# Two transformer blocks on one Trainium2 core: the second block on tokens that aren't normed, first gathers routed by one head

## The reference

```python
def second_block(x, ...):
    xn = rmsnorm(x, norm1_w); proj = xn @ w_in
    gq, gk, gv, ggate, gr, mq, mk, mv = jnp.split(proj, offsets, axis=-1)
    log_a = log_sigmoid(gr @ gla_w_alpha + gla_b_alpha) / 16
    o_gla = rmsnorm(gla_chunked(gq, gk, gv, log_a), gla_out_norm_w) * silu(ggate)
    qh, kh = rope(rmsnorm(mq, q_norm_w)), rope(rmsnorm(mk, k_norm_w))   # 8 heads of 64
    mixed = concatenate([o_gla, moba_attention(qh, kh, mv)]) * mix_scale
    x = x + mixed @ w_out
    return x + peer_ffn(rmsnorm(x, norm2_w), w_query, subkeys, u_tab, v_tab)
def peer_ffn(xt, ...):
    q = (xt @ w_query).reshape(T, 8, 2, 128); s = einsum('thpd,hpkd->thpk', q, subkeys)
    sv, si = top_k(s, 16)                       # best 16 of 128 keys, per head and half
    cand = sv[:, :, 0, :, None] + sv[:, :, 1, None, :]     # 256 candidates
    top_s, pos = top_k(cand, 16); expert = cand_id[pos]; gate = softmax(top_s)
    act = gelu(einsum('thkd,td->thk', u_tab[expert], xt))
    return einsum('thk,thkd->td', gate * act, v_tab[expert])
```

## Time and profile before

| what | us |
|---|---|
| median of 3 runs (lowest, highest) | 1672.82 (1672.74, 1673.08) |
| profiled execution, its own time | 1673.72 |
| its span | 1671.9 |
| TensorE busy | 1479.3 (88%) |
| VectorE busy | 786.0 (47%) |
| ScalarE busy | 267.4 (16%) |
| POOL busy | 308.8 (18%) |

### The profile page before, as it was taken

One profiled execution on the slowest core, in us unless ns is written; L12 is line 12 of the kernel. 1 busy time (PEld: TensorE's weight loads), 2 busy tenths in 40 slices (PEclk: granted clock), 3 DMA queues, 4 the chain that ended last, 5 costly groups with the idle time before them and its releaser, 6 DMA issues.

```text
span 1671.9 us, 17113 instructions
## 1 busy us (share of the span) xinstructions
PE 1479.3 (88%) x6432; PEld 810.1 (48%) x6432; DVE 786.0 (47%) x1839; ACT 267.4 (16%) x651; POOL 308.8 (18%) x288
## 2 busy tenths in 40 slices
PE   6999999899999999999699798898787778887768
PEld 5897885644444434443446575553333333333323
DVE  2216754522232323222333466376767676666544
ACT  1312221100000000000133321222212121212111
POOL 0001000100000000000000012355444444444441
PEclk9999999999999999999799899999989998989999
DMA  9532347399999999999405138899999999999996
GB/s 372 238 121 89 144 152 302 132 407 427 428 428 427 428 427 428 425 429 427 194 29 224 51 139 304 312 366 422 421 422 422 421 422 420 423 422 421 422 421 278
DMA packets 60274, 551.08 MB, mean 330 GB/s; under 512 B 8608, under 2 KB 8896, under 8 KB 10400
## 3 DMA queue, kind: packets, MB, share of 16 engines
q1 hardware_dynamic: 22192, 277.47, 40.1%
q0 software_dynamic: 38000, 272.50, 39.8%
HBM read 548.90 MB, written 1.05 MB: 329 GB/s over the span
## 4 chain that ended last, share of the span: by engine, by line
PE 46%; DMA 42%; issue 5%; DVE 4%; ACT 2%; POOL 2%; SPq 1%; DVEq 0%; POOLq 0%
DMA ring<-expert_w_d 17%; DMA ring<-peer_uv_d,work 17%; PE ps L1497 8%; PE ps L1134 8%; DMA consts_sb<-peer_uv_d,work 7%; PE ps L1746 6%; PE ps L1244 5%; PE ps L1128 5%; PE ps L1605 4%; DMA ring<-w_ada_d 2%; PE ps L1401 1%; PE ps L1536 1%; POOL ring L1881 1%; PE ps L1142 1%; PE ps L1481 1%
## 5 line engine op out<-in xcount | busy, mean ns | idle before, releaser
L1746 PE MATMUL ps<-ring,work 128*128 128x512 f32 x752 | 366.1, 641 | 93.7 <-ACT work L1077 93.7
L1746 PEld LDWEIGHTS ps<-ring,work 128*128 128x128 f32 x752 | 150.3, 205 | 303.9 <-issue 180.8
L2767 DVE CUSTOM_DVE_ANT_0 ring<-ring,work 128x1024 f32<-128x1024 f32 x188 | 229.7, 1223 | 129.1 <-DMA ring<-peer_uv_d,work 127.7
L1881 POOL DMA_INDIRECT ring<-peer_uv_d,work x188 | 209.1, 1112 | 280.4 <-PE ps L1746 190.6
L1497 PE MATMUL ps<-ring,work 128*64 128x512 f32 x1024 | 225.4, 593 | 10.2 <-DMA ring<-expert_w_d 9.4
L1497 PEld LDWEIGHTS ps<-ring,work 128*64 128x64 f32 x1024 | 78.0, 137 | 154.3 <-issue 153.2
L1077 ACT ACTIVATE work<-consts_sb,work 128x128 f32<-128x128 f32 x256 | 82.7, 390 | 259.8 <-DVE work L2776 256.0
L1134 PE MATMUL ps<-ring,hT 128*128 128x512 f32 (+1 forms) x288 | 122.6, 584 | 1.7 <-issue 0.8
L1536 PE MATMUL ps<-ring,work 128*64 128x512 f32 x512 | 113.4, 595 | 0.7 <-DVE work L2397 0.7
L1746 PE MATMUL ps<-work 128*128 128x512 f32 x136 | 74.1, 672 | 35.0 <-ACT work L1077 34.9
L2393 DVE TENSOR_TENSOR work<-work,ps 128x512 f32<-128x512 f32 x16 | 11.0, 687 | 198.8 <-PE ps L1497 198.8
(11 more groups left out here) (392 smaller groups left out, 1520.5 us busy)
## 6 DMA issues: line engine op xcount, KB each, us to landing
ring<-expert_w_d SPq DMA_DIRECT2D x96, 2048.0 KB, 15.7
ring<-w_in_d SPq DMA_DIRECT2D x13, 2048.0 KB, 18.0
ring<-w_ada_d SPq DMA_DIRECT2D x12, 2048.0 KB, 8.9
ring<-w_out_d SPq DMA_DIRECT2D x4, 2048.0 KB, 8.4
ring<-peer_w_query_d SPq DMA_DIRECT2D x4, 2048.0 KB, 7.8
ring<-peer_uv_d,work POOLq DMA_INDIRECT x188, 22.7
mod<-b_ada_d SPq DMA_DIRECT2D x1, 2048.0 KB, 25.9
consts_sb<-consts_d SPq DMA_DIRECT2D x1, 1346.0 KB, 24.9
```

What stands on the lines that cost most here:

```text
L1746: last = pe.matmul(ps[V_BANK[t] + n][:, :], diag[:, i % 4, :], v_row(i)[:, n * 512:(n + 1) * 512], start=(i % (16 * PH) == 0), stop=(i % ( ...
L1881: pool.indirect_dma_start(out=uv_rows(i), out_offset=None, in_=io["peer_uv"], in_offset=bass.IndirectOffsetOnAxis(ap=idx[:, s, k:k + 1], a ...
L2767: dve.tensor_tensor_reduce(out=u_row(i), in0=u_row(i), in1=h_tok[:, i // (16 * PH), :], scale=1.0, scalar=0.0, op0=ALU.mult, op1=ALU.add, ...
```

## The change

Block two: x is transposed as it is. Final norm and norm1 weights are multiplied into one column per 128 features (`cols1`) and applied when the transposed tokens are copied out of PSUM (`features_in`, `scaled_in`); the factor of each token (`s_of`, both norms in one, made from sums of squares of x and of x times the final norm's weight) is applied behind the products, by the engine that empties the bank. Features by tokens (gr, gqk) get it as a row: job sr turns it, `row_s` holds it. norm2 likewise: `cols2` in front, the token's factor behind the key scores. The normed x itself (`residual`) is made while the products run.

The order of block two: xT00, xT01 and query 0 stand in front of the second half's attention values. The first route is done by one head, then the other (`head` in `route`), and `idx_ready` counts heads. Weights come in batches of 2 for the first 64 picks. The late queries stand in quarters between pairs of picks (`query_part`, `STEPS`), key scores as a fifth step. The places are freed in another order, and one (15) waits for a semaphore `row_used`.

Block one: the modulation is made in two halves with half of the key product between; lengths are summed by products with a matrix of ones that leave them spread over all rows (jobs lk, lq), rooted on ScalarE and inverted as 128x512 on VectorE; G, B and X are made by transposing; ScalarE empties X.

```diff
-    for name in ("k0", "k1", "gab", "q0", "q1", "v0", "v1", "ss"):
+    for name in ("gab", "q0", "q1", "v0", "v1"):
         add(name, "D")
-    for name in ("cx", "nq"):
+    for name in ("lk0", "lk1", "lq0", "lq1", "cx", "nq"):
         add(name, "A")
-    for name in ("rk0", "rk1", "rq0", "rq1"):
-        add(name, "D")
+    add("gc", "D")
     for name in ("nk", "nv"):
         add(name, "A")
-    add("gc", "D")
...
+LATE_QUERIES = ((0, 2), (1, 0), (1, 1), (1, 2), (0, 3), (1, 3))
+STEPS = 5
...
-    steps = [("go11", (12, 13)), ("yT10", (14,)), ("wo10", (0, 1)), ("wo11", (2, 3)), ("xT10", (15,)), 4,
-             ("q10", (4, 5)), 8, ("q11", (6, 7)), 12, ("q12", (8, 9)), 20, ("q13", (10, 11)), n]
+    done = {q: 2 * (STEPS * j + 4) for j, q in enumerate(LATE_QUERIES)}
+    steps = [("q00", (13,)), ("go11", (12,)), ("yT10", (14,)), ("wo10", (0, 1)), 2, ("wo11", (2, 3)), ("row", (15,))]
+    for i in range(4):
+        steps += [done[(1, i)], (f"q1{i}", (4 + 2 * i, 5 + 2 * i))]
+    steps.append(n)
...
-    return [(i, BATCH) for i in range(0, n - 8, BATCH)] + [(i, 1) for i in range(n - 8, n)]
+    return ([(i, 2) for i in range(0, EARLY, 2)] + [(i, BATCH) for i in range(EARLY, n - 8, BATCH)]
+            + [(i, 1) for i in range(n - 8, n)])
...
+            modulation(0)
+            warm(8)
+            modulation(2)
+            columns(0)
+            warm(6)
...
+            key_chunk(6, 0, 0, 0)
+            key_chunk(6, P, T, 0)
+            modulation(1)
+            evacuated("xT3")
+            key_chunk(7, 2 * P, 0, 0)
+            key_chunk(7, 3 * P, T, 0)
+            modulation(3)
+            columns(1)
             warm(10)
...
-                for d, tri in ((0, u_inc), (1, l_inc)):
-                    heads(f"G{t}{d}", lambda h: gg[:, t, d * 4 + h:d * 4 + h + 1].to_broadcast([P, P]), lambda h: tri)
+                for d in range(2):
+                    turned(f"G{t}{d}", lambda h: gcum[:, t, d * 4 + h:d * 4 + h + 1].to_broadcast([P, P]))
...
-                    if lv < LEVELS - 1:
-                        heads(f"X{lv}{t}{d}", lambda h: XT[d][:, t, h, :], lambda h: tU[d][:, t, h, :])
+                    evacuated(f"Y{lv - 1}{t}{d}" if lv > 1 else f"tr{t}{d}")
                     heads(f"Y{lv}{t}{d}", lambda h: tU[d][:, t, h, :], lambda h: XT[d][:, t, h, :])
+                if lv < LEVELS - 1:
+                    for t, d in CHAINS:
+                        evacuated(f"Y{lv}{t}{d}")
+                        turned(f"X{lv}{t}{d}", lambda h: XT[d][:, t, h, :])
...
+            for name, c0 in (("lk0", 4), ("lk1", 6), ("lq0", 0), ("lq1", 2)):
+                dve.wait_ge(ev_a, head_evacuated(name))
+                gv2 = g_cv[:, c0:c0 + 2, :]
+                o(dve.reciprocal(sq[:, c0:c0 + 2, :], sq[:, c0:c0 + 2, :]))
+                sync()
+                dve.tensor_tensor(gv2, gv2, sq[:, c0:c0 + 2, :], ALU.mult).then_inc(len_ready, 1)
...
-            pe.wait_ge(tok_ready, 1)
-            to_features("nT", 0, h_tok)
+            pe.wait_ge(moe_done, 1)
+            to_features("nT", 0, x)
...
-            values(0, 4)
-            for i, (t, g) in enumerate(((1, 0), (1, 1), (1, 2), (0, 3), (1, 3))):
-                query(t, g)
-                values(4 * i + 4, 4 * i + 8)
-                key_scores(t, g)
+            at = 4
+            for j, (t, g) in enumerate(LATE_QUERIES):
+                for c in range(STEPS):
+                    values(at, max(at, 2 * (STEPS * j + c + 1)))
+                    at = max(at, 2 * (STEPS * j + c + 1))
+                    if c < 4:
+                        query_part(t, g, c)
+                    else:
+                        key_scores(t, g)
...
             bsync()
-            routes(0, 0, 2)
+            routes(0, 0, 2, 0)
+            gla_masked(1)
+            routes(0, 2, 5, 0)
+            turned_p(1, 0)
+            turned_p(1, 2)
+            routes(0, 5, 11, 0)
+            gla_state(2)
             moba_out(1)
-            routes(0, 2, 6)
+            routes(0, 11, 22, 0)
             gla_out(1)
-            routes(0, 6, 14)
+            routes(0, 0, 5, 1)
             features_in("yT", 1, 1)
-            routes(0, 14, PARTS)
-            out_added(1)
-            for i in range(4):
+            routes(0, 22, PARTS, 0)
+            routes(0, 5, 12, 1)
...
+                if i == 2:
+                    out_added(1, 0)
+                if i == 4:
+                    out_added(1, 1)
+                    squares(1, 5)
+                    scaled_in("xT", 1, cols2)
...
+                if i == 6:
+                    row_normed()
```

648 lines of the change are left out of this document (379 added, 269 removed).

## The result

| kernel | median us (lowest, highest) | runs |
|---|---|---|
| before | 1672.78 (1672.70, 1673.08) | 4 |
| changed | 1630.82 (1628.33, 1631.10) | 4 |

The changed kernel is faster: ratio 0.9746, 95% interval 0.9729 to 0.9762, so 42.0 us. The forecast was 1613 (59.8 us gained) in a range of 1598 to 1633: the direction and the range held, but 18 us of the expected gain did not come.

What follows compares the result with a forecast made beforehand. TensorE and DMA were taken to bound the kernel about equally, in turns. Block one 16.8, first gather 37.3 and behind it 5.2 sum to 59.3 us off 1673.72: 1614.4, as median 1613; range 1598 to 1633.

Steps and rivals of the forecast that it cites:

- Block one: TensorE's path through the first block, busy without a gap from 37 to 165 us: 16.8 us gained in all.
- The lengths: Block one: four products of ones replace one-column sums of squares and row scales; 4.6 us gained.
- The levels: Block one, inversion levels 1 to 5: X made by transposing, 20 groups at 0.445 us less; 8.9 us gained.
- G and B: Block one: decay and beta rows by transposing, eight groups; 3.6 us gained, 1.5 taken off for clock.
- the wait: Block one: TensorE waits for VectorE's four 128x512 reciprocals, 3.8 us each; 5.0 us lost.
- The first transposes: Start of block two: TensorE transposes x once the last expert is added, at 797.3 us, without the earlier 12.65 idle.
- the projections: Block two: the first two projections, 16.33 us after idle time, return to 13.97 at full clock; 2.4 us gained.
- The search and the first gather: Block two: key scores at 932.7 us, one head's routing 9.8 plus 5.7 other work, first gather at 949.2.
- 37.3 us for the first gather: Block two's path: the first gather starts at 949.2 us, 37.3 earlier, counted as gain in the sum.
- Behind the first gather: DMA engines lose 23.2 us up to pick 9, none after, where 28.4 were lost before; 5.2 us gained.
- the loop does not close: Rival, chance 0.09: 8 places too few even in pairs, picks 9 to 58 lose 41 us; up to 1654.
- the slower one: Rival, chance 0.02: POOL's in-order wait makes rounds of 8 places exceed 3.7 us a pick; 60 us lost, 1675.

Runs made afterwards that it cites:

- no_branch: Changed kernel with TensorE's branch around the experts removed, only the usual way kept: 1619.39 us (kernel before on that chip 1672.66).
- mended_warm: Changed kernel with usual way last in branch, norm row's place later, reciprocals earlier; plus 13 unread products in two TensorE waits: 1618.17 us (1617.59 without them).
- both_heads: Changed kernel with both heads of the first tile routed before the first gather: 1625.11 us (changed kernel on that chip 1625.37).
- row_later: Changed kernel with the norm weight's row as the place of pick 11, not of pick 9: 1624.40 us.
- changed_again: The changed kernel itself, unaltered, measured a second time: 1625.37 us (first measurement 1630.82).
- mended_pairs: Changed kernel with usual way last in branch, norm row's place later, reciprocals earlier; plus weights in pairs for 128 picks, not 64: 1612.49 us (1617.59 without).

## Why the prediction was right or wrong

**Block one: right, term by term.** Forecast 16.8 us, measured 17.6. The keys ended at 46.33 (forecast 46.7). The lengths: 3.44 us where 8.1 were (4.54 + 3.57), so 4.7 against 4.6. The 64 records behind them gained 2.4 (2.3), though in this execution the 32 and 128 records before the lengths lost 0.8 each to a lower clock. The levels, from their first product to the end of the fifth: 76.2 us before (164.73 to 240.89), 67.0 after (156.27 to 223.29), so 9.1 (8.9). G and B: the second half's group took 4.4 us for 6.2, the first half's 6.1 for 6.3 at a lower clock behind the wait; 2.0 against 3.6 - 1.5. Only the wait was mis-sized: 3.05 us, not 5.0, because one reciprocal took 3.35 us and not 3.8:

```profile
100.38 3.35 DVE L2135 RECIPROCAL ring<-ring 128x512 f32<-128x512 f32 x1 [0.21 <-DVE small L2129]
```

That is 6.5 ns a column; the slope from 8 to 16 columns had given 7.2. The estimate of 4.3 us from the Trainium skill, "VectorE: DVE Perf Modes", section "Walkthrough: the 8-slice pipeline in each mode", was further off.

**The first transposes: the step that failed first.** The prediction had "Now it transposes x as soon as the last expert is added". It was wrong by 6.1 us, and the projections ("that goes too (2.4)") kept 1.9 us of theirs, as TensorE again stood idle in front of them. `no_branch` shows the cause: TensorE's branch. The kernel before has the same branch at the same place, and there the jump fits inside the 12.65 us in which TensorE waited for the norms, so that the trace had no row for it; that is read from its code, no run takes the branch out of that kernel. I read those 12.65 us as VectorE's alone, and asked what hides each edit but not what that wait was hiding. The Trainium skill, "Runtime: NRT & Kernel Launch", section "Instruction fetch mechanics", says that a taken branch to code outside the window held by the engine makes it wait for a DMA fetch; the gaps agree with it (6.1 us with the DMA engines at 421 GB/s, up to 2 us at the entry, with 2 GB/s). That the time is the fetch itself no run here shows; that it is the branch, `no_branch` does. The rule stood there to be weighed before. A small slip comes on top: the 17.4 us forecast for the second half's first projection is 0.3 to 0.4 more than its three terms (11.5, 2.4 and 3.2) give.

**The search and the first gather: right in kind, 2.1 us short.** From the first key scores to the first gather it took 18.6 us, forecast 16.5. VectorE stood 2.47 us waiting for the attention values, which took 6.10 us at half clock instead of 3.7. Before them the order had gained 1.2 us more than forecast. The low clock goes on behind the values; first two stretches of the changed kernel, then two of the kernel before with the same work:

```profile
930.00:940.00 10.00, 10.00 (x41) 8.65 (x40) 6.72 (x21) 0.90 (x5) 0.00 (x0) 0.50 0.00 0
940.00:950.00 10.00, 10.00 (x60) 9.55 (x60) 4.57 (x20) 2.48 (x7) 1.97 (x2) 0.67 0.61 211
```

```profile
960.00:970.00 10.00, 9.85 (x77) 8.55 (x76) 7.19 (x34) 1.60 (x7) 0.00 (x0) 1.00 0.01 2
970.00:980.00 10.00, 9.20 (x80) 8.80 (x79) 7.94 (x33) 3.87 (x10) 0.00 (x0) 1.00 0.00 0
```

The values, the state products and the next query took 23.0 us (928.48 to 951.49), before 15.1 (962.09 to 977.20). The prediction had no term for these 7.9 us. They lie on the way to pick 2, which waits for y turned behind that query: it came 13.4 us behind the first gather, not 7.7. What the time would be at full clock no run shows, since `mended_warm` did not bring the clock back.

**What the first gather is worth: wrong reading, small harm.** The sum listed 37.3 us for the first gather and then took back what the engines stand still. `both_heads` shows that only the second half of this counts: the start can move by 7.75 us and the time doesn't. What counts is when the places behind pick 1 come free, which by POOL's rows is TensorE's chain through the turned y, the output projection and the first value products (picks 2 to 8) and then VectorE's norm (pick 9).

**Behind the first gather: wrong by 7.7 us.** The prediction had "From pick 9 on I expect no more hole", and 23.2 us lost. Its own sign of being wrong, a rate below 400 GB/s between 978 and 1080 us, showed (the first row). By the rates (421 GB/s when full), the losses are those of the rows behind it:

```profile
978.00:1080.00 102.00, 89.06 (x383) 54.57 (x382) 63.99 (x197) 23.48 (x64) 40.93 (x38) 0.95 0.94 374
...
941.00:991.00 50.00, 43.97 (x198) 29.15 (x198) 29.74 (x94) 14.84 (x33) 12.65 (x12) 0.94 0.57 201
991.00:1060.00 69.00, 60.20 (x243) 35.58 (x242) 39.22 (x110) 14.12 (x37) 26.33 (x27) 0.93 0.99 392
...
1130.00:1190.00 60.00, 51.18 (x167) 26.72 (x166) 43.73 (x124) 12.87 (x38) 30.92 (x27) 0.94 0.97 390
1190.00:1615.00 425.00, 339.50 (x698) 139.93 (x697) 272.08 (x675) 77.99 (x234) 183.99 (x166) 0.92 1.01 421
```

50 x (1 - 201/421) = 26.1, then 4.8, and 4.4 from 1130 to 1190: 35.3 us, where the kernel before lost 31.5 in the same way (302 GB/s for 50 us, 322 for 74). The prediction counted 28.4 for the kernel before and thought none would be left behind pick 9, where 9.2 were. Up to pick 9, 2.9 more were lost than forecast. The row's place, which costs about as much (`row_later`), is not the reason, as the prediction had the wait for it; picks 2 to 8 came 4 to 8 us later behind the first gather than forecast. Of the 4.8 us, some 3 belong to this execution: `changed_again` took 3.2 us less from the first expert product to pick 32. The last 4.4 hold the step from pairs to fours at pick 64, which the prediction never looked at (`mended_pairs`, 2.8 us). The loop itself does close: from 1060 to 1130 us the engines moved 421 GB/s, and in `changed_again` 406 and 418 already from 1010 to 1040 and to 1070. With whole queries a hole of 5.1 us comes first, then 421. So the rival "the loop does not close", by which picks 9 to 58 keep 314 GB/s, was not it, nor was the slower one.

The terms of the miss: 6.1 + 1.9 - 1.2 + 2.1 + 7.7 = 16.6 us, of the 16.5 between 59.3 and 42.8. The other 1.3 us between 1613 and 1630.8 is the rounding at the ends: the median now lay beside the profiled run, not 0.9 below it. How much of the miss is this one measurement is open to 5 us: the second time the median was 1625.4. That the time fell inside the range is no proof of the account: the range was drawn for the reciprocals, the clock and starved gathers, and the largest miss, the jump, was in none of these.

## What to carry to other kernels

When an edit takes away a long wait, ask what else happened inside it: a jump, a table, a transfer that no row shows because the wait covered it. Where a branch is unavoidable, let the usual way be the one that runs straight on into the code that is waited for. And where a queue of transfers fills slowly, count how many can be out at a time, and when their places come free; here moving only the first one earlier moved nothing.

## What the runs showed of the hardware that was not expected

- A jump of TensorE over one loop's code cost 5.6 to 6.1 us of idle time at the end of a stage with the DMA engines full, and 1.4 to 2.0 us where they were nearly idle (2 GB/s).
- The granted clock fell to 0.83 of 2.4 GHz between 40 and 60 us although TensorE was busy there without a gap and since 24 us had not stood idle for more than 0.4 us, in one execution and not in the next; the same 128 records took 30.38, 29.54 and 27.87 us in three traces. This is 2.5 of the 7.4 us between two executions of one kernel.
- A reciprocal of 128x512 takes 3.35 us on VectorE, five times an ordinary operation of that size (0.69).
